# State-space decays from the second chunk on, made from split running sums that ACT shapes

## What is computed

```python
adt = dt * a                                  # per token and head
a_cs = cumsum(adt, axis=-1)                   # running sum inside a chunk
seg = a_cs[..., :, None] - a_cs[..., None, :]
lmat = exp(where(causal, seg, -inf))          # 128 x 128 per head and chunk
cb = einsum('bclgn,bcsgn->bcgls', cc, bc)
y_diag = einsum('bcgels,bcsgep->bclgep', cb[:, :, :, None] * lmat, xdt)
decay_states = exp(a_cs[..., -1:] - a_cs)
states = einsum('bclgn,bcgel,bclgep->bcgepn', bc, decay_states, xdt)
# running state over the chunks (new_states), then
y_off = einsum('bclgn,bcgepn,bcgel->bclgep', cc, prev_states, exp(a_cs))
y = y_diag + y_off + xh * d_skip              # gated by silu(z), normed by group
```

## Time and profile before

| | us |
|---|---|
| median of 3 runs | 2368.07 |
| the profiled execution, its own time | 2367.63 |
| its span in the trace | 2365.9 |
| end of the projection, from the first transpose to the mixer's start (1579.0 to 1588.8) | 9.80 |
| the mixer up to the products for the next one (1588.8 to 1705.1) | 116.3 |

### The profile page before, as it was taken

The page is one execution under the profiler, slowest core; times in us unless marked ns, Lnnn a source line. Parts: engine busy times, 40 slices in busy tenths (PEclk is TensorE's granted clock), DMA queues, the critical chain, the costliest instruction groups (busy, mean ns, idle before and its releaser), DMA issues. The chain is left out here.

```text
span 2365.9 us, 26688 instructions
## 1 busy us (share of the span) xinstructions
PE 2224.6 (94%) x10482; PEld 1657.8 (70%) x10482; DVE 1369.5 (58%) x2047; ACT 803.6 (34%) x1358; POOL 360.8 (15%) x263
## 2 busy tenths in 40 slices
PE   6999988886999999999999889998998999997999
PEld 3454764465778888888888668995667977443887
DVE  3859556656798655555455675318846287575210
ACT  3100112353473233334444353334454333345110
POOL 1000000031124422220000100016300000364000
PEclk9999989877999999999999999999999999997999
DMA  7540007404353322226534221100132110103231
GB/s 273 163 140 9 27 31 239 166 1 131 100 170 102 103 81 81 85 73 249 194 122 134 72 80 47 36 1 18 63 85 72 36 38 17 72 20 121 71 88 55
DMA packets 215427, 216.75 MB, mean 92 GB/s; under 512 B 18850, under 2 KB 171738, under 8 KB 214376
## 3 DMA queue, kind: packets, MB, share of 16 engines
q1 hardware_dynamic: 200076, 196.57, 26.4%
q0 software_dynamic: 3344, 12.58, 1.4%
q10 hardware_dynamic: 11884, 5.91, 0.9%
HBM read 172.12 MB, written 41.74 MB: 90 GB/s over the span
## 5 line engine op out<-in xcount | busy, mean ns | idle before, releaser
L2269 PE MATMUL bk_in<-t_part,a 128*128 128x512 f32 x1272 | 294.6, 390 | 1.3 <-DVE arena L2738 0.9
L2269 PEld LDWEIGHTS bk_in<-t_part,a 128*128 128x128 f32 x1272 | 238.4, 188 | 53.2 <-issue 3.0
L2288 PE MATMUL bk_in<-hid_part,b_part 128*128 128x512 f32 x1056 | 242.0, 391 | 3.1 <-DVE b_part L2618 3.1
L2288 PEld LDWEIGHTS bk_in<-hid_part,b_part 128*128 128x128 f32 x1056 | 198.0, 188 | 46.4 <-DVE b_part L2618 3.9
L991 PE MATMUL fr_ps<-arena,work 128*128 128x512 f32 x384 | 168.9, 601 | 5.0 <-DMA work<-in_w_in 5.0
L4444 PE MATMUL fo_ps<-fo_hi,fo_part 128*128 128x512 f32 x512 | 161.9, 395 | 6.8 <-DVE fo_lo L4488 6.8
L3066 PE MATMUL bk_in<-h_part,sj_part 128*128 128x512 f32 x576 | 135.9, 396 | 6.7 <-DVE h_part L2773 5.3
L3615 PE MATMUL aj_ps<-h_part,aj_part 128*128 128x512 f32 x576 | 141.7, 402 | 0.0
L991 PEld LDWEIGHTS fr_ps<-arena,work 128*128 128x128 f32 x384 | 73.6, 193 | 96.6 <-issue 91.5
L2269 PE MATMUL bk_out<-t_part,a 128*128 128x512 f32 x576 | 134.8, 389 | 0.0
L3066 PEld LDWEIGHTS bk_in<-h_part,sj_part 128*128 128x128 f32 x576 | 108.3, 189 | 33.8 <-issue 6.2
(11 more groups left out here) (656 smaller groups left out, 3979.9 us busy)
## 6 DMA issues: line engine op xcount, KB each, us to landing
work<-in_w_mod SPq DMA_DIRECT2D x24, 1024.0 KB, 8.0
w_raw<-in_w_ffn_out SPq DMA_DIRECT2D x43, 512.0 KB, 3.7
work<-in_w_in SPq DMA_DIRECT2D x25, 512.0 KB, 3.9
g_raw<-in_w_ffn_in SPq DMA_DIRECT2D x24, 512.0 KB, 3.8
hid_raw<-kept_hid SPq DMA_DIRECT2D x22, 512.0 KB, 4.9
w_raw<-in_w_in SPq DMA_DIRECT2D x20, 512.0 KB, 3.8
w_raw<-in_w_out SPq DMA_DIRECT2D x16, 512.0 KB, 3.8
work<-in_w_out SPq DMA_DIRECT2D x8, 1024.0 KB, 7.0
```

What stands on the lines that cost most here:

```text
L2269: mm = pe.matmul(bank, ring[n % 4][a][:, k, :], moving[:, b, k, :], start=(opens and k == 0 and j == 0), stop=(k == HK - 1 and j == 2), sk ...
L2288: mm = pe.matmul(pi[:, m, :], w_part[n % 2][:, a, at:at + P], hid_part[k][:, b, :], start=(k == 0 and j == 0), stop=(k == FT - 1 and j == 2))
```

## The change

The kernel keeps the first chunk's `R` and its float32 matmul. It is written into the place of the `xc` tiles 4 and 5 and not 0 and 1, so that GpSimd waits for 12 turned jobs and not 4. From the second chunk on there is no `R`, and GpSimd has three operations in a pass.

In place of `R`, the running sums themselves are used. ACT copies them out of `pt` once more, without the exponential. At the end of the projection DVE makes five small operations on the identity (`rows_of`), columns that pick rows, and between its third and fourth copies (`cums_in_parts`) it rounds the sums to fp32r (`hi`), clears a tile of 128 x 1024 and writes four strided parts into it: hi, sum - hi, -hi and hi - sum.

In the mixer, PE transposes one 128 x 128 tile of these parts for each chunk (`cums_of`), into one of the three `pa` banks. ACT makes five operations of 128 x 128 from it (`parts_of`), with a scale and a bias for each partition: `lead` and the four pieces of `trail`, both rounded. The exponents of a group q are then one fp32r matmul over 32 partitions (rows 32q to 32q + 31) in place of the float32 one over 128, and the matmul with -1e30 as before. Two tiles each of `lead` and `trail` take turns.

The rest of the diff gives `scan` of a later stage (the attention's projection) over to the semaphore `made`, with its counts moved by one.

```diff
@@ class SsdProjection
-        self.R = A.view(XC0, SSD_H, P)
+        self.R = A.view(XC0 + 4 * T, SSD_H, P)
+        S.ss_cum_hi = rounded(nc, S, "ss_cum_hi", SM0 + 768, NT, SSD_H)
+        S.ss_cums, S.ss_pick = A.view(XC0, NT, 4, 32), A.view(M_SMALL + 280, 42)
...
-        pe.wait_ge(s.ea, 3)
+        pe.wait_ge(s.ea, 4)
...
+                nc.scalar.activation(V.e, self.pt[:, 0, 0:P].rearrange("p (c h) -> p c h", h=SSD_H), ACT.Copy)\
+                    .then_inc(s.ea, 1)
...
-        pool.wait_ge(s.turned, 4)
+        pool.wait_ge(s.turned, 12)
...
+    def rows_of(self, step):
+        nc, S, s = self.nc, self.S, self.s
+        one = S.ss_pick[:, 0:32]
+        step(nc.vector.tensor_reduce(one, S.ident.rearrange("p (q j) -> p j q", q=4), AX, ALU.add))
+        nc.vector.tensor_tensor(S.ss_pick[:, 32:36], one[:, 0:4], one[:, 4:8], ALU.add)
+        nc.vector.tensor_tensor(S.ss_pick[:, 36:40], one[:, 8:12], one[:, 12:16], ALU.add)
+        nc.vector.tensor_reduce(S.ss_pick[:, 40:41], one[:, 8:16], AX, ALU.add)
+        nc.vector.tensor_reduce(S.ss_pick[:, 41:42], one[:, 0:8], AX, ALU.add)
+
+    def cums_in_parts(self, dve, step):
+        nc, S, s = self.nc, self.S, self.s
+        cum = self.V.e.rearrange("p c (q h) -> p c q h", h=4)
+        hi = S.ss_cum_hi[:, :, :].bitcast(F32).rearrange("p c (q h) -> p c q h", h=4)
+        to = lambda n: S.ss_cums[:, :, :, 4 * n:4 * n + 4]
+        dve.wait_ge(s.ea, 4)
+        nc.vector.tensor_copy(S.ss_cum_hi[:, :, :], self.V.e)
+        step(nc.vector.memset(S.ss_cums, 0.0))
+        nc.vector.tensor_copy(to(0), hi)
+        nc.vector.tensor_tensor(to(1), cum, hi, ALU.subtract)
+        nc.vector.tensor_scalar(to(2), hi, -1.0, None, ALU.mult)
+        nc.vector.tensor_tensor(to(3), hi, cum, ALU.subtract)
...
+        self.rows_of(step)
         for n, (m, h) in enumerate(self.jobs):
+            if n == 6:
+                self.cums_in_parts(dve, step)
@@ stage_ssd
-    R = A.view(at, SSD_H, P)
+    cums, pick = S.ss_cums, S.ss_pick
+    lead = [rounded(nc, S, f"ss_lead{i}", SM0 + 640 + i * P, P) for i in range(2)]
+    trail = [rounded(nc, S, f"ss_trail{i}", at + T + i * HALF, 4, P) for i in range(2)]
+    R = A.view(at + 4 * T, SSD_H, P)
...
+        for kind, c in [("seg", 0), ("cum", 1), ("cum", 2), ("seg", 1), ("seg", 2)] + \
+                [(kind, c) for c in range(3, NC) for kind in ("cum", "seg")]:
+            if kind == "cum":
+                takes(cum_bank, c, s.parts, c)
+            else:
+                for q in range(4):
+                    takes(seg_bank, 4 * c + q, s.E, 4 * c + q + 1)
...
-                        pool.wait_ge(s.seg, 4 * c + 4)
-                        pool.tensor_tensor(R, S.t_le.unsqueeze(1).broadcast_to([P, SSD_H, P]),
-                                           adt[:, c + 1, :].unsqueeze(2).broadcast_to([P, SSD_H, P]), ALU.mult)\
-                            .then_inc(s.R, 1)
...
+                def free(bank):
+                    if bank >= 3:
+                        pe.wait_ge(*freed[bank - 3])
+
+                def cums_of(c):
+                    free(cum_bank[c])
+                    pe.transpose(pa[:, cum_bank[c] % 3, 0:P], cums[:, c, :, :].rearrange("p q j -> p (q j)"), S.ident)\
+                        .then_inc(s.cum, 1)
...
-                        pe.wait_ge(s.R, c)
+                        pe.wait_ge(s.parts, c)
                     for q in range(4):
-                        u = 4 * c + q
-                        if u >= 3:
-                            pe.wait_ge(s.E, u - 2)
-                        pe.matmul(pa[:, u % 3, :], S.t_gt, R[:, 4 * q:4 * q + 4, :].rearrange("p h l -> p (h l)"),
-                                  start=True, stop=False)
...
+                        bank, rows = seg_bank[4 * c + q], slice(32 * q, 32 * q + 32)
+                        free(bank)
+                        if c:
+                            pe.matmul(pa[:, bank % 3, :], lead[c % 2][rows, :],
+                                      trail[c % 2][rows, :, :].rearrange("p h l -> p (h l)"), start=True, stop=False)
...
                 decays(0)
+                cums_of(1)
                 for c in range(NC):
                     tok = slice(c * P, (c + 1) * P)
+                    if c + 2 < NC:
+                        cums_of(c + 2)
...
+                def parts_of(c):
+                    act.wait_ge(s.cum, c)
+                    if c >= 3:
+                        act.wait_ge(s.seg, 4 * c - 4)
+                    turned = pa[:, cum_bank[c] % 3, 0:P]
+                    nc.scalar.activation(lead[c % 2][:, :], turned, ACT.Identity, scale=pick[:, 40:41], bias=pick[:, 41:42])
+                    for h in range(4):
+                        k = nc.scalar.activation(trail[c % 2][:, h, :], turned, ACT.Identity, scale=pick[:, 32 + h:33 + h],
+                                                 bias=pick[:, 36 + h:37 + h])
+                    k.then_inc(s.parts, 1)
...
                 decays(0)
+                parts_of(1)
+                parts_of(2)
                 decays(1)
                 for c in range(NC):
                     if c + 2 < NC:
+                        if c:
+                            parts_of(c + 2)
                         decays(c + 2)
```

More of the change, by code:

```diff
@@ L3534, in stage_project_att @@
         s = semaphores(nc, S, ctx, "aj", "r0 r1 hi lo done free bias act exped dve logs rows squared mean eps root made"
-                                         " normed scan wiped copied scores late logits x turned mr")
+                                         " normed wiped copied scores late logits x turned mr")
         ps = psum(nc, ctx, "aj_ps", 4, PSB)
@@ L3584, in maxima @@
                         pe.wait_ge(s.copied, 3)
-                        pe.wait_ge(s.made, 2)
+                        pe.wait_ge(s.made, 3)
                     if k == turn_after:
@@ L3628, in _ @@
                     if m == 4:
-                        pe.wait_ge(s.scan, 1)
+                        pe.wait_ge(s.made, 1)
                         for i in range(NT):
@@ L3704, in _ @@
             def _(pool):
-                pool.wait_ge(s.scan, 1)
+                pool.wait_ge(s.made, 1)
                 pool.memset(S.ones_r[:, :].bitcast(F32), 1.0)
@@ L3752, in _ @@
                         nc.vector.tensor_tensor_scan(S.crow, one, pr[0:ATT_H, :, :].rearrange("p a b -> p (a b)"), 0.0,
-                                                     ALU.mult, ALU.add).then_inc(s.scan, 1)
-                        dve.wait_ge(s.scan, 1)
+                                                     ALU.mult, ALU.add).then_inc(s.made, 1)
+                        dve.wait_ge(s.made, 1)
                         nc.vector.tensor_scalar(S.late, S.t_ge, -1.0, 1e30, ALU.add, ALU.mult)
@@ L3766, in _ @@
                 nc.vector.tensor_copy(S.c_r[0:8, :], S.crow).then_inc(s.made, 1)
-                dve.wait_ge(s.made, 1)
+                dve.wait_ge(s.made, 2)
                 for at in (0, 64):
@@ L4114, in stage_ssd @@
         S.ssd_sent = semaphores(nc, S, S.past_ssd, "sz", "sent")
-        s = semaphores(nc, S, ctx, "ss", "consts R skip xdt xds G seg E M offs decayed added Y summed y_ok kept st_mm"
+        s = semaphores(nc, S, ctx, "ss", "consts cum parts skip xdt xds G seg E M offs decayed added Y summed y_ok kept st_mm"
                                       " upd sq ms root inv diag turned outa outd")
@@ L4118, in stage_ssd, with takes @@
         pg = psum(nc, ctx, "ss_g", PSB)
+        freed, cum_bank, seg_bank = [], {}, {}
+        def takes(table, n, *until):
+            table[n] = len(freed)
+            freed.append(until)
+        for kind, c in [("seg", 0), ("cum", 1), ("cum", 2), ("seg", 1), ("seg", 2)] + \
[5 more added lines that the diff above has]
+                    takes(seg_bank, 4 * c + q, s.E, 4 * c + q + 1)
         pd = psum(nc, ctx, "ss_d", 2, PSB)
@@ L4162, in decays @@
                     if c:
-                        pe.wait_ge(s.R, c)
+                        pe.wait_ge(s.parts, c)
                     for q in range(4):
-                        u = 4 * c + q
-                        if u >= 3:
-                            pe.wait_ge(s.E, u - 2)
-                        pe.matmul(pa[:, u % 3, :], S.t_gt, R[:, 4 * q:4 * q + 4, :].rearrange("p h l -> p (h l)"),
-                                  start=True, stop=False)
-                        pe.matmul(pa[:, u % 3, :].rearrange("p (h l) -> p h l", l=P), ident_r[:, :],
+                        bank, rows = seg_bank[4 * c + q], slice(32 * q, 32 * q + 32)
[3 more added lines that the diff above has]
+                                      trail[c % 2][rows, :, :].rearrange("p h l -> p (h l)"), start=True, stop=False)
+                        else:
+                            pe.matmul(pa[:, bank % 3, :], S.t_gt, R[:, 4 * q:4 * q + 4, :].rearrange("p h l -> p (h l)"),
+                                      start=True, stop=False)
```

(3 more changed lines are left out.)

## The result

The changed kernel takes 2353.35 us, the median of 5 runs (2351.84 to 2360.16). The kernel before, in turns with it, takes 2369.75 (2367.85 to 2370.55). The ratio is 0.9944, with a 95% interval of 0.9932 to 0.9956. It is faster, by 13.3 us going by the ratio and by 16.4 going by the two medians, where 22.8 was forecast. The time lies inside the stated range of 2339 to 2356, near its dear end.

A forecast was written before the change was run, and what follows sets the result against it. PE and DVE were both taken as full in the mixer, with R holding both. The mixer loses 24.3 us, the projection's end adds 1.5: 22.8 less, so 2345 us, range 2339 to 2356.

The forecast's parts named there:

- What bounds the kernel now: Mixer: PE and DVE both full in middle windows; R makes PE wait 2.96 us, holds DVE, and costs a float32 matmul.
- The group of exponents: PE in a steady mixer pass: each group falls from 1.09 to 0.46 us, so four save 2.52.
- PE's sum of 11.35: PE's work in a steady mixer pass: 13.76 less 2.52 plus 0.11 for the added transpose; 11.6 us with waits.
- 71.0 for the windows: Six mixer windows between state updates: 13.5 + 4 x 11.6 + 11.1 = 71.0 us, from 93.48.
- c = 6: Last of the six mixer windows between state updates, without exponents to make: forecast 11.1 us, 10.61 before.
- c = 1: First of the six mixer windows between state updates: forecast 13.5 us, 21.76 before.
- Rival 1: Mixer: DVE stays the bound, held by GpSimd's skip, xdt and xds; pass 13.6 us, kernel 2354; chance 0.21.
- Rival 2: Mixer: a group over 32 partitions keeps its 1.09 us; pass 13.8 to 14, kernel 2360; chance 0.05.
- Rival 3: Mixer: PE's clock drops from 2.4 to 1.2 GHz for the stage, 68 us over six passes, kernel 2413; chance 0.04.
- Rival 4: Mixer: the four new matmuls overlap their neighbours, up to 0.9 us less per pass, kernel 2341; chance 0.07.
- End of the projection: Before the mixer: DVE's added operations cost 1.5 us (0.8 to 2.5); R stays hidden by 0.6, otherwise up to about 1.
- ACT's parts: Steady mixer pass: five added ACT operations cost 1.4 to 1.9 us in sum, covered before PE needs them.

The follow-up runs named there:

- experiment 3: The kernel before, without GpSimd's R from the second chunk on, float32 matmuls kept (decays wrong, for timing only): 2356.47 us, one run.
- experiment 1: The changed kernel with the new exponents matmul reading all 128 partitions instead of 32 (exponents wrong, for timing only): 2348.58 us, one run.
- experiment 5: The changed kernel with ACT writing four zero-masked leads, so the new matmul runs over 128 rows with the same sums: 2343.83 us, one run.
- experiment 9: The changed kernel with zero-masked leads over 128 rows, a reordered projection end and parts made at DVE's eighth copy: 2341.80 us, ratio 0.9894 to the kernel before.
- experiment 4: The changed kernel with GpSimd's skip waiting for DVE's mean instead of ACT's squares: 2362.76 us, one run.
- experiment 2: The changed kernel with the 32-row matmuls of two groups side by side, then their two bounds: 2350.30 us, one run.
- in 8: The changed kernel with paired 32-row matmuls, a reordered projection end and skip behind DVE's mean: 2351.58 us, ratio 0.9929 to the kernel before.

## Why the prediction was right and wrong

- **What bounds the kernel now: right.** R cost three times over. Without it alone (experiment 3) the mixer is 11.0 shorter, the hold of the state's decay and PE's wait for R are gone, and PE's own sum of 13.76 shows as 13.58.
- **The group of exponents: the step that failed.** The term "four groups save 2.52" took the 0.23 of a matmul in a long row of equals, and measured it is (1.09 - 0.855) x 4 = 0.94. PE's sum of 11.35 becomes 12.93 with it, and 12.77 was measured. The row that I leaned on, 396 ns over 40 partitions against 390 over 128, told how long a record is, and where the 40 partitions stand, between matmuls over 64, the loads are hidden: it was no row for a place between matmuls over 128. The sum had no term for a weight load and took it as hidden in every case. What the runs showed in its place is starts 0.43 apart, of which 0.19 are a load in the open. With equal rows (experiments 1, 5, 9) the sum holds: 11.23 against 11.35 for PE, 69.92 against 71.0 for the windows.
- **The bookkeeping.** The mixer is 8.3 short of the forecast. Three steady windows are 1.2 longer each (3.5; of the fifth, 14.31, that is without its spell), the spell is 1.5, c = 6 is 1.9, c = 1 0.6, the first update 0.9, and c = 2 gives back 0.1. The 3.5 goes with the weight loads: with equal rows these windows are 11.81, 11.23 and 11.30 (experiment 5). c = 6 comes to 11.23 with masked leads, 1.77 less. DVE's list splits that: 0.93 up to the right half of the output (L4376), of which 0.31 and 0.42 are waits for the late exponentials, and 0.83 from there to the decay of `offs` (L4400), where `mean` takes 1.42 against 0.79.
- **Rival 1, DVE held by GpSimd.** Its time, 2354, is what was measured, by luck: its mechanism isn't the cause. The hold is there (1.42 against 0.15), and taking it away leaves the window at 12.77 (experiment 4). Whether it counts once PE is at 11.2 isn't shown: there moving `skip` makes it worse (12.10), since the hold goes from a small operation to the decay of the state.
- **Rival 2, PE not shorter,** was half true: a group kept 0.855 of its 1.09, for a reason that the rival didn't have.
- **Rival 3, the clock,** came in small. There is no stage at 1.2 GHz, but spells of some 3 us, each 1.5 to 1.7 us dear. I had tied the clock to waits, by the record behind the 2.96; of the spells in the 14 traces eleven stand at or behind a wait and seven don't (last section).
- **Rival 4, overlap with neighbours:** no. Matmuls over different groups of 32 rows do run beside each other (experiment 2), but none ran beside one over 128.
- **End of the projection: right in the part that was worked out, short in the cover.** PE's waits came to 1.65 against 1.5. The other 1.1 is R: "it stays hidden by 0.6 us" counted its end against the opening of the barrier. In the trace the barrier opens 1.73 after GpSimd's last operation, where in experiment 9, with GpSimd long done, it opens 0.27 after ACT's. "If R's cover is gone, up to about 1 us" was the bound that came true.
- **ACT's parts: right.** 0.44 and 1.49 are 1.9 us (the upper end), begun at 1642.52, and PE never waits for them. PE never waits for GpSimd at the exponents, as said.
- **What wasn't in the sum:** the 3.87 us ahead of the projection's end. Unchanged or nearly unchanged code took from 1576.9 to 1582.8 us up to that point in the 14 traces, so a comparison of two single runs is open by several us there, while stage lengths repeat to 0.1 at equal clock.

## What to carry to other kernels

A matmul that reads fewer rows is no cheaper when its neighbours read more: price it by the distance between starts in that very neighbourhood, and if its weight load shows, pad it to full rows with zeros or put equals side by side. Before an operation is moved so that it no longer holds another engine, ask which of that engine's operations it will hold next, and whether that engine is the bound at all. Compare stages by their windows and clocks, since whole times of single runs here differ by more than the edits do.

## What was not expected of the hardware

- A weight load at a change between a 32-row and a 128-row rounded matmul isn't hidden: starts 0.43 apart against 0.23 among equals, at 512 columns. It was seen in both directions. Between 40 and 64 partitions it was hidden.
- The granted clock fell while PE was busy throughout. In the changed kernel PE was busy for every microsecond of the two windows ahead (12.78 of 12.78, 12.76 of 12.76), and then:

```profile
1661.20:1662.20 1.00, 1.00 (x3) 0.38 (x3) 1.00 (x2) 0.75 (x2) 0.66 (x1) 1.00 0.00 0
1662.20:1663.20 1.00, 1.00 (x4) 0.42 (x3) 0.73 (x2) 0.74 (x2) 0.00 (x0) 0.97 0.00 0
1663.20:1664.20 1.00, 1.00 (x5) 0.91 (x5) 0.71 (x1) 0.45 (x2) 0.00 (x0) 0.50 0.00 0
...
1666.20:1667.20 1.00, 1.00 (x8) 0.97 (x8) 0.13 (x1) 0.13 (x1) 1.00 (x1) 0.83 0.00 0
1667.20:1668.20 1.00, 1.00 (x3) 0.38 (x2) 0.63 (x2) 1.00 (x4) 0.92 (x2) 1.00 0.00 0
```

  That is 1.2 GHz for some 3 us, and 2.4 GHz around them. The mixers of the 14 traces have 18 such spells. The kernels with 32-row matmuls one by one have one, three, three and four, that with pairs two and none (in 8), those with 128 rows none, none, none, one, one and two, the kernel before one and experiment 3 none. They are of two kinds. Eleven begin within or up to 1.2 us behind a wait of PE of 1.64 to 2.96 us; but twelve other waits of 1.65 to 2.53 us have none behind them. The other seven have no wait above 0.9 us ahead of them, and all seven are in the four traces with 32-row matmuls one by one: each begins between 0 and 0.9 us after the start of the last of the eight matmuls of the exponents (here L4225 at 1663.15). So the exposed loads are the obvious suspect, since a part of "busy" is a load and no matmul; but most such passes have no spell, and why one has it stays open. The Trainium skill ("TensorE: Matmul & The Clock Gate", section "What's actually happening") has the clock throttled when PE is idle and released by activity; no row here shows PE idle ahead of this fall.
- GpSimd's last operation and the opening of the barrier are 1.73 us apart (1593.67 to 1595.40), ACT's last operation and its first behind the barrier 0.27 when GpSimd had long been done (experiment 9). In the changed kernel ACT ended 0.34 after R and still waited 1.37.
- A copy of 128x128 on DVE took 1.37 us beside GpSimd's R and 0.23 without it, and an operation on 128x2 1.42 beside `skip` and 0.15 without: in each case the small operation ended within 0.1 us of the large one.
